# Moving one tile's scan ahead of the next tile's input coefficients in a state-space mixer

## The reference, cut to what matters

```
lam_bar = exp(lam * dt)
b_bar = ((lam_bar - 1.0) / lam)[..., None] * b_c
bu = einsum("blgh,gph->blgp", u, b_bar)
x[t] = lam_bar * x[t-1] + bu[t]            # over all 512 positions
y = einsum("blgp,ghp->blgh", x, c).real + d * u
ys = gelu(y);  y_ssm = (ys * sigmoid(ys @ w_ssm_glu)) @ w_ssm_o
```

## Time and profile before

| | us |
|---|---|
| median of 3 runs | 2910.63 (2910.57 to 2911.03) |
| span of the profiled execution, first to last instruction | 2909.3 |
| state-space part of layer 0 (from its first step 0 to the last "cb" product) | about 83 to 279 |
| state-space part of layer 1 | about 1009 to 1202 |

### The profile page before, as it was taken

The page is one execution under the profiler, slowest core; times in us unless marked ns, Lnnn a source line. Parts: engine busy times, 40 slices in busy tenths (PEclk is TensorE's granted clock), DMA queues, the critical chain, the costliest instruction groups (busy, mean ns, idle before and its releaser), DMA issues.

```text
span 2909.3 us, 31864 instructions
## 1 busy us (share of the span) xinstructions
PE 2580.0 (89%) x12117; PEld 2054.5 (71%) x12117; DVE 1531.0 (53%) x2304; ACT 635.2 (22%) x1257; POOL 1463.2 (50%) x994
## 2 busy tenths in 40 slices
PE   4788898989999888899999999978976688699998
PEld 3677667868888677676777878866744457578887
DVE  7775443545345477644443252354688863565433
ACT  2111442110000121254011010031145561310000
POOL 4232455756666532354665656663432235366664
PEclk9899899999999999999999999988987689999999
DMA  3221122322222222121232222232110001122222
GB/s 124 61 66 48 62 73 72 106 82 101 94 97 90 92 71 66 48 77 66 84 105 97 99 87 94 90 106 78 57 35 1 1 1 62 55 80 94 94 99 83
DMA packets 80135, 217.97 MB, mean 75 GB/s; under 512 B 15728, under 2 KB 25328, under 8 KB 79472
## 3 DMA queue, kind: packets, MB, share of 16 engines
q1 hardware_dynamic: 60912, 200.96, 20.7%
q10 hardware_dynamic: 19072, 14.98, 1.9%
HBM read 207.25 MB, written 2.10 MB: 72 GB/s over the span
## 4 chain that ended last, share of the span: by engine, by line
PE 71%; DVE 22%; ACT 3%; issue 2%; ACTq 0%; DMA 0%; POOL 0%; DVEq 0%
PE psG L840 21%; PE psG L841 20%; PE psG L842 20%; DVE tmp L1633 3%; DVE work_b L1633 3%; DVE work_m L1633 3%; PE psO L1006 1%; DVE b_lo L1633 1%; DVE work_m L1843 1%; DVE stats L1913 1%; DVE work_b L2031 1%; DVE max L2030 1%; DVE work_b L1636 1%; PE psT L950 1%; PE psO L1072 1%
## 5 line engine op out<-in xcount | busy, mean ns | idle before, releaser
L784 POOL TENSOR_SCALAR w_hi<-w_raw 128x1024 fp32r<-128x1024 f32 (+4 forms) x417 | 414.5, 994 | 1131.2 <-PE psG L842 1118.8
L786 POOL TENSOR_TENSOR w_lo<-w_raw,w_hi 128x1024 fp32r<-128x1024 f32 (+4 forms) x417 | 945.8, 2268 | 34.8
L840 PE MATMUL psG<-h_hi,w_hi 128*128 128x512 f32 x1944 | 784.6, 404 | 26.6 <-DVE h_lo L1677 17.9
L841 PE MATMUL psG<-h_lo,w_hi 128*128 128x512 f32 x1944 | 768.7, 395 | 0.0
L842 PE MATMUL psG<-h_hi,w_lo 128*128 128x512 f32 x1944 | 767.2, 395 | 0.0
L840 PEld LDWEIGHTS psG<-h_hi,w_hi 128*128 128x128 f32 x1944 | 372.3, 192 | 128.8 <-issue 42.4
L842 PEld LDWEIGHTS psG<-h_hi,w_lo 128*128 128x128 f32 x1944 | 372.0, 191 | 80.1
L841 PEld LDWEIGHTS psG<-h_lo,w_hi 128*128 128x128 f32 x1944 | 372.5, 192 | 77.7 <-issue 3.0
L1633 DVE TENSOR_TENSOR x<-x,psG 128x512 f32<-128x512 f32 x112 | 77.0, 688 | 426.4 <-PE psG L842 426.4
L840 PE MATMUL psG<-m_hi,w_hi 128*128 128x512 f32 x736 | 287.3, 390 | 3.5 <-DVE m_lo L1633 3.5
L841 PE MATMUL psG<-m_lo,w_hi 128*128 128x512 f32 x736 | 286.5, 389 | 0.0
(11 more groups left out here) (273 smaller groups left out, 3082.2 us busy)
## 6 DMA issues: line engine op xcount, KB each, us to landing
w_raw<-wstream SPq DMA_DIRECT2D x327, 512.0 KB, 3.2
w_raw<-wstream SPq DMA_DIRECT2D x64, 256.0 KB, 2.6
w_raw<-wstream SPq DMA_DIRECT2D x16, 384.0 KB, 3.0
work_b<-work_b ACTq DMA_DIRECT2D x16, 256.0 KB, 5.4
work_b<-cmpw ACTq DMA_DIRECT2D x2, 2048.0 KB, 7.7
x<-xT SPq DMA_DIRECT2D x4, 512.0 KB, 6.2
small_work<-ssmp ACTq DMA_DIRECT2D x8, 256.0 KB, 3.4
outT<-x SPq DMA_DIRECT2D x1, 2048.0 KB, 6.3
```

The source lines that it names most:

```text
L784: pool.tensor_scalar(hi, w, 1.0, 0.0, ALU.mult, ALU.add).then_inc(s_hi, 1)
L786: pool.tensor_tensor(lo, w, hi.bitcast(F32), ALU.subtract).then_inc(s_split, 1)
L840: pe.matmul(out, whi, hi, start=(k == 0), stop=False)
L841: pe.matmul(out, whi, lo, start=False, stop=False)
```

## The change

In the plan, step 1 follows step 0 at once; the product that stood between them stands between steps 2 and 3, so that there are two. Four products still go with every tile. On VectorE, `build_inputs` of tile f+1 leaves step 1 and stands at the head of step 3, ahead of the wait for the outputs of step 3 and of `build_outputs`. It gets one more wait, for wt_sb.

```diff
@@ mixer_plan
     ahead = 3 if l == 0 else 2
+    last_step = 3
     for key in first:
         if key[0] not in ("rot", "vt"):
             if products >= ahead and t <= SSM_LAST:
-                plan.append(("ssm", t))
-                t += 1
+                if last_step == 2:
+                    last_step = -1
+                else:
+                    plan.append(("ssm", t))
+                    last_step = t % 4
+                    t += 1
+                    if last_step == 0:
+                        plan.append(("ssm", t))
+                        last_step = 1
+                        t += 1
             products += 1
         plan.append(("job", key))
@@ VectorE, ssm_step
-                elif phase == 1 and ft + 1 < FEATURE_TILES:
-                    dve.wait_ge(s_toep, 16 * SSM_T * (f + 1))
-                    build_inputs(f + 1, pwork)
                 elif phase == 2 and ft < FEATURE_TILES:
                     states(f)
                 elif phase == 3 and ft + 1 < FEATURE_TILES:
+                    dve.wait_ge(s_toep, 16 * SSM_T * (f + 1))
+                    dve.wait_ge(v["wt_sb"], f + 1)
+                    build_inputs(f + 1, pwork)
                     dve.wait_ge(v["yc"], f + 1)
                     build_outputs(f + 1, pwork)
```

## The result

The changed kernel takes 2941.16 us (median of 4 runs, 2938.4 to 2944.29), the one before beside it 2910.83 (2910.57 to 2911.19): ratio 1.0105, 95% interval 1.0091 to 1.0119. It is 30 us slower. I had forecast 8 us more, with 2933 us as the upper end.

The account below looks back on a forecast made before the run. TensorE, busy 89% of the span, was taken as the bound. Removed 65 us, added 53.4 of waits + 20 of clock = 73.4: 8.4 us slower, 2919 us; 8-in-10 range 2900 to 2933.

Parts of the forecast that it names:

- The waits before step 3 and their slow clock: TensorE's eight waits for `states` and the slow step 3s behind them all go: 42.6 + 17 = 60 us removed.
- The tail of layer 0: End of layer 0: first glu product no longer waits for splits, attention chain starts earlier; 5 us removed, bounds 0 and 9.
- Wait A: Added before step 2: ug_sb comes late behind ScalarE's DMA issues; 29.5 us over eight tiles.
- Wait B: Added before line 916: w1 comes late from VectorE's `build_inputs` and `build_outputs`, 3.0 us of it split blocking; 23.9 us in all.
- Rival 1: Faster, 2902 us: splits and `build_outputs` don't block each other where they meet; chance 0.15.
- The clock: Slow clock behind the added waits: 10 us for four B waits, 10 us (0 to 20) for eight A waits.
- Rival 2: The clock falls at every A wait: 10 us more, 2929 us; chance 0.13.
- Rival 3: TensorE still waits at step 3, `states` late or scans blocked: 16 us, with the clock 2935 or more; chance 0.05.
- Rival 4: The moved product simply pays: w1 isn't late before line 916, only A stays; 2885 us, chance 0.05.
- Rival 5: No change to tell, several rivals at once: 2905 to 2916 us; chance 0.12.

Follow-up runs that it names:

- no_a: Changed kernel with ScalarE's eight Toeplitz DMA issues moved from step 0 to behind the input copy of step 1: 2889.12 us, 0.9924 of the kernel before.
- no_b: Changed kernel with `build_inputs` moved from the head of step 3 to the end of step 2, behind `states`: 2910.49 us, 0.9996 of the kernel before.
- plan_only: Kernel before with the new plan alone, `build_inputs` left in step 1: 2908.52 us, 0.9983 of the kernel before.
- fill_a: Changed kernel with 12 unread matmuls put into each wait before step 2: 2918.33 us, 1.0020 of the kernel before.
- fill_b: Changed kernel with 18 unread matmuls in each of the four long waits before line 925: 2930.24 us, 1.0068 of the kernel before.

## Why the prediction was wrong, step by step

**The waits before step 3 and their slow clock: right.** 42.6 and 17 us went; no wait before line 959, eight step 3 of 5.45 us.

**The tail of layer 0: right in size.** The first attention transpose came 18.5 us after the first attention scores before (279.04 to 297.49) and 13.2 after (293.42 to 306.64), 5.2 us less against 5. The size was right, the reason only in part: 3.3 us are the two waits of the first glu product, which are gone, and about 1.7 are a low stretch of 3.4 us behind them (before, 286.5 to 290.0, PEclk 0.51) that the prediction didn't have. The wait of the transpose itself did not shrink, 6.04 before and 6.64 after:

```profile
306.64 0.69 PE L995 MATMUL psT<-consts,work_m 128*128 128x128 f32 x2 [6.64 <-DVE work_m L1649]
```

**Wait A: right in size.** Forecast 3.9, 3.1, 4.0, 3.4 and 4.4, 3.1, 3.4, 4.2; measured 4.3, 2.4, 2.7 (before line 939, released by ypre), 3.0 and 3.9, 2.9, 3.0, 2.0 + 1.4: 25.5 us against 29.5. The cause is as told for six of them and part of a seventh, ScalarE's issues (no_a). The 2.7 us and the 2.0 came by ypre in place of ug_sb, and the 2.7 stand unchanged in no_a. (The terms shown in the prediction, 11.0 or 11.7 less 7.0 or 7.9, would give 3.8 to 4.7 a tile, up to 0.8 above the list; the rows behind the list aren't shown.)

**Wait B: right in size.** Forecast 0, 5.2, 0, 7.0 and 0, 5.3, 5.5, 0.9; measured 0, 4.8, 0, 6.6 and 0, 4.8, 5.2, 1.2: 22.5 us against 23.9. The price of a `build_outputs` operation beside a split, which no row had, is this, VectorE and GpSimd after:

```profile
133.92 1.52 DVE L1642 TENSOR_TENSOR work_b<-work_b,work_m 128x576 f32<-128x576 f32 x1
135.47 2.78 DVE L1642 TENSOR_TENSOR work_b<-small_work,work_b 128x576 f32<-128x576 f32 x1
138.28 0.76 DVE L1642 TENSOR_TENSOR work_m<-small_work,work_b 128x576 f32<-128x576 f32 x1
...
134.92 2.72 POOL L795 TENSOR_TENSOR w_lo<-w_raw,w_hi 128x1024 fp32r<-128x1024 f32 x1
```

The two cost 2.8 us over 0.76 each; I had taken 3.0. The operation of 2.78 us ends 0.6 us after the split's 137.64. The Trainium skill (SBUF — State Buffer, "SBUF: two separate sides") calls the pair of ports that VectorE and GpSimd share an exclusive lock. The trace agrees, as the blocked operation ends about its own length after the split. Rival 1 needed under 1.5 us here and falls.

**The clock: wrong, and here alone the error lies.** The step was: "The eight A waits lie at 3 to 4.4, between the rows' 0.9 and 4.1: 0 to 20 us; I take half, 10." Two things in it failed.

First, the share. In the changed kernel not half of these waits but all eight were followed by 1.2 GHz, those of 2.4, 2.7 and 3.0 us too. The seven rows of before that I had held only 4.1 us and more, and one of 0.9: they didn't forbid it, and I read the gap between as even odds. Rival 2 had this, and stood at 0.13.

Second, the price. I took 2.5 us for each, which was step 3's. It is no constant of a wait: it is what TensorE does next, twice as long, until the clock is back. Behind seven of these waits come step 2, line 907 and in tile 0 the first third of a product, and the low level lasts 11.9 us there where it lasted 5.4 behind a wait before line 925. The eight are worth 36.4 us of busy time (changed kernel less no_a), 4.6 each; the low stretches behind them in the changed kernel's own trace, about 72 us in all at half clock, give 36 too. So the term was 36 where I had 10, and even its upper bound of 20, which was also rival 2's, was 16 too low.

For B the term was about right: no_a still has its B waits and a busy time of 336.2, against 328.4 for the same matmuls without the 17 us of before (345.4 - 17): 8 us, where I had 10. The two terms are not independent, and the split depends on what is taken away first. no_b, which has little of B, has a busy time of 27.2 us over the same 328.4; so the A waits cost 27 us of clock with little of B and 36 with all of it, 3.4 to 4.6 each, and about 9 us come only when both kinds are there. On either count A's term is where the loss lies. The Trainium skill (TensorE: Matmul & The Clock Gate, "HAM oscillation — how this bites in real kernels") tells of a loop in which a gap in every turn brings the low clock back in every turn, so that the transition is paid as often as the loop turns. This trace agrees: the mean granted clock of layer 0's part is 0.86 with the gaps before step 2 and 0.96 in no_a.

With the measured terms the ledger reads: removed 42.7 + 17 + 5.2, added 25.5 + 22.5 + 8 + 36.4, which is 27.5 us, where the forecast ledger gave 8.4: the clock behind A is 26.4 more, and A, B and B's clock together are 7.4 less. The span grew by 33.2. The other 5.7, of which about 3 are the profiled run's distance from the median, are outside the ledger: layer 0's part began 1.4 us later, between its end and layer 1's start 3.7 more were lost than the tail explains (728.6 us against 730.1, where 5.2 less was due), and 0.8 behind layer 1. Kernels with the same plan lie between 724.7 (plan_only) and 730.3 (no_b) in that stretch, so I can't say what sets it. Two slips in the prediction's arithmetic changed nothing: with the A clock at 0 and the tail at 9 the low end is 2905, not 2908, and the split of the earlier trace rows is 1.4 us over its usual length, not 1.7.

**The rivals.** Rival 2 is what came, with a price nearly twice as high as the 20 us that it gave. Rivals 1, 3, 4 and 5 fall: blocking is as large as priced, step 3 doesn't wait, line 925 does.

## What to carry to other kernels

A wait can cost its length and then the difference between the two clocks over what follows until the clock is back; price it by what stands behind it, not by what an earlier wait cost elsewhere. If small matmuls follow, that can be more than the wait itself, as here 3.4 to 4.6 us behind waits of 3.2 on average. Before two steps are joined, look at what the engine between them has in its own queue ahead of the one result that the second step needs: here 5.6 us of DMA issues in front of a copy of 0.6, and moving them behind it turned a change that lost 1.05% into one that gains 0.76% (with `build_inputs` behind `states` as well, 1.07%).

## What was not expected of the hardware

- The length of a wait alone doesn't tell whether the clock falls. In the changed kernel waits of 2.4 to 3.0 us were each followed by 1.2 GHz, and in fill_a, tile 0, step 2 had a mean clock of 0.78 behind 1.25 us of standing. But the 0.9 us before a step 3 and 0.5 us in fill_b did nothing, the same 2.7 us before line 939 that had a low stretch behind it in the changed kernel had none in no_a, and in no_b one wait of 2.5 us before a step 2 of layer 1 left the clock whole, as this window of that step 2 shows; one of 2.15 us in plan_only did too. The runs don't tell what parts these from the others.

```profile
1069.97:1073.76 3.79, 3.79 (x34) 3.79 (x35) 1.52 (x2) 2.48 (x3) 0.28 (x1) 1.00 0.68 204
```

- The clock can fall while TensorE is at work. Step 2 in tile 3 of layer 1 of the changed kernel ran its first 2.2 us at full clock, behind waits of 2.0 and 1.4 us, and the rest at half (in fill_a, tile 0, it fell after 2.5 us of step 2):

```profile
1187.79:1190.01 2.22, 2.22 (x20) 2.22 (x20) 2.19 (x2) 0.61 (x1) 2.22 (x1) 1.00 0.03 7
1190.01:1192.84 2.83, 2.83 (x15) 2.83 (x15) 0.64 (x1) 0.00 (x0) 0.09 (x1) 0.51 0.51 184
```

- In the changed kernel a wait before step 2 with matmuls in it that compute nothing was cheaper than the wait alone: 96 of them took 23 us off, and 128 that stood wholly in the way, behind the waits, cost 2.5 us, since they gave back nearly all that they took.
- The line of fill_b that answers to it, TensorE at line 925 (928 there) behind 18 fillers and what was left of a 4.8 us wait:

```profile
138.71 1.92 PE L928 MATMUL psS<-work_b 128*16 128x128 f32 x16 [0.53 <-DVE work_b L1645]
```
